# A two-block sequence model in f32 on one core: the attention stage with two heads on row halves, the rotated part on row strips, and score groups set between transposes and value products

## The chip, the cores and the metric

One Trainium2 chip, one of its cores. The metric is the device time of one execution in microseconds (us), the median of several runs. All data are f32. Engines: PE (TensorE: matmuls and transposes; PEld is its weight load), DVE (VectorE), ACT (ScalarE), POOL (GpSimd), SP (the queue that issues most DMAs). Every f32 matmul stands in the trace as two records of PE (two passes over the same columns) and two of PEld; a transpose is one record of each.

## The reference, cut to what matters

The program runs two layers one after the other over 2048 tokens of width 1024. The first (two gated linear recurrences, a gated merge) and the second layer's gates, spatial mixing and output product are not touched. The change is in the second layer's causal attention: 8 heads, 64 plain and 32 rotated channels for each query and key (96 in all), 64 channels of value.

```python
q = einsum('bsr,re->bse', rmsnorm(c_q, q_norm_g), w_uq).reshape(b, s, 8, 96)
q_nope, q_rope = q[..., :64], rope(q[..., 64:], positions)
kv = einsum('bsr,re->bse', rmsnorm(c_kv, kv_norm_g), w_ukv).reshape(b, s, 8, 128)
k_nope, val = kv[..., :64], kv[..., 64:]
k_r = broadcast(rope(k_rope, positions), 8 heads)      # one rotated key for all heads
qf, kf = concat([q_nope, q_rope]), concat([k_nope, k_r])
# for each block of queries:
sc = einsum('bqhd,bkhd->bhqk', qf, kf) / sqrt(96)
sc = where(kpos <= qpos, sc, -inf)
p = softmax(sc); o = einsum('bhqk,bkhd->bqhd', p, val)
```

## The kernel before

`build` calls one phase after another; each ends before the next begins. `phase_latents` makes the latent vectors of queries and keys (`cqT`, `ckvT`), the rotated queries (to memory, `queries_rotated`), the rotated key and the values `vall`. `phase_attention` follows, then `phase_output`.

`phase_attention` takes the heads in four pairs `a`. For a pair it projects the 64 plain channels of queries and keys of both heads (L3302, L3306: 4 blocks of 512 tokens) into PSUM banks; ACT copies each head's 64 rows to rows 0 to 63 of `qT` and `kT` (L3379). Rows 64 to 95 hold the rotated part: of `qT` by DMA (L3285), of `kT` written by DVE in `phase_latents` (L3161, twice per block). So one matmul over 96 rows makes one score tile.

A block `p` (0 to 7) of a pair is 256 query rows: two heads `e` by two row tiles `r` of 128, against 2p+1+r chunks of 128 keys. Two pieces of work belong to a block:

- scores, "S": for each of the four tiles (`TILES`), its keys in pieces of up to 512. PE makes a piece in one of three banks (`NS`, L3319); DVE scales it into `sc` and keeps the row maximum (L3439), adds the mask to the last 128 keys (L3444), and forms the maximum (L3448, L3451). ACT then takes the exponential of the whole tile in place, with its row sum (L3388).
- the rest, "R": for each chunk of keys PE transposes the four 128x128 squares into one of three banks (`NTB`, L3334); DVE or ACT copies the bank to `pT` (L3462, L3399); PE multiplies the values by it, one head on output columns 0 to 63 and the other on 64 to 127 (L3347). Transposes go in groups of four chunks (`GROUP`); the value products of a group follow the transposes of the next. At the end PE spreads the reciprocal sums over the columns (L3361), ACT copies them (L3405) and DVE scales the output (L3464).

The order is a list written by hand, the same for all engines: per pair the projections, then S of block 7, R of the previous pair's block 3, S 0, R 7, S 6, R 0, S 1, R 6, S 5, R 1, S 2, R 5, S 4, R 2, S 3, R 4. A large block's S is followed by a small block's S and so on, so that DVE and ACT work on one block while PE works through another. Which engine copies a transposed chunk is set by `by_vector`: DVE for all chunks of blocks 0 to 3 and the odd chunks of 4 to 7, ACT for the even ones.

"Switch" is used below for a point at which PE goes from matmuls on the whole array to matmuls on a part of its rows or columns, or back, or from one such part size to another.

Of the kernel before, what the change touches and what calls it, by code (L numbers as in the profile page):

```python
# [18 lines left out]
P = 128  # L19
BANK = 512  # L20
# [2889 lines left out]
def phase_latents(chip, hT, positions, inv_freq, w_in, w_uq, q_norm_g, kv_norm_g, cqT, ckvT, kT, qr_d, WV, w_ukv, wv_saved, vall,  # L2910
# [9 lines left out]
    with ExitStack() as st:  # L2920
# [24 lines left out]
        D = Stages(sem("dve_stage"), "vq vkv inv q0 q1 kv krc krs kr0 kr1")  # L2945
# [146 lines left out]
        def _(dve):  # L3092
# [43 lines left out]
            for b in range(NB):  # L3136
# [5 lines left out]
                if b:  # L3142
                    dve.wait_ge(D.sem, D.at(b - 1, "kr1"))
# [16 lines left out]
                for e in range(2):  # L3160
                    dve.tensor_tensor(kT[R, e, t], kr[R, 0, :], kr[R, 1, :], ALU.add).then_inc(D(f"kr{e}"), 1)  # L3161
# [3 lines left out]
def phase_attention(chip, cqT, ckvT, kT, w_uq, w_ukv, qr_d, qr_stored, vall, oT, extra, w_out, wo_saved):  # L3165
# [6 lines left out]
    NS, NTB = 3, 3  # L3172
    GROUP = 4
    NPT = 2 * GROUP
    SC0, TB0, OB0 = 0, 3, 6
    BIG, SMALL = QT // 2 - 1, QT // 4 - 1
    with ExitStack() as st:
# [4 lines left out]
        qT = sb("qT", [QK, 2, SEQ])  # L3182
        ahead = sb("ahead", [P, P])
        sc = [sb("sc_big", [P, 2, (4 * BIG + 3) * P]), sb("sc_small", [P, 2, (4 * SMALL + 3) * P])]
# [5 lines left out]

        order = []
        for a in range(PAIRS):
            order += [("P", a, 0), ("S", a, 7)] + ([("R", a - 1, 3)] if a else [])
            order += [(x, a, p) for x, p in (("S", 0), ("R", 7), ("S", 6), ("R", 0), ("S", 1), ("R", 6), ("S", 5), ("R", 1),
                                            ("S", 2), ("R", 5), ("S", 4), ("R", 2), ("S", 3), ("R", 4))]
        order.append(("R", PAIRS - 1, 3))
        TILES = [(e, r) for e in range(2) for r in range(2)]
        slot = lambda p: 0 if p > SMALL else 1
        length = lambda p, r: 2 * p + 1 + r
        pieces = lambda p, r: (length(p, r) + 3) // 4  # L3200
        chunks = lambda p: range(2 * p + 2)

        score_names, turn_names = [], []
        for x, a, p in order:
            if x == "P":
                score_names += [f"{k}{a}_{b}" for b in range(NB) for k in "qk"]
            elif x == "S":
# [38 lines left out]
        def wait_evicted(eng, name):  # L3246
            done = DT if turned_of[name] else AT
            eng.wait_ge(done.sem, done.at(0, name))
# [576 lines left out]
```

## Time and profile before

| what | value |
|---|---|
| median of 3 runs | 3966.22 us (3966.11 to 3969.06) |
| profiled execution: span from first to last instruction (no other time of it is given) | 3966.9 us |
| PE busy over the span | 3738.9 us, 94% |
| attention stage, first projection to last output scaling | 3142.95 to 3748.7 us |
| DVE, ACT busy in 3146 to 3752 | 366.5 us, 267.8 us of 606 |
| one pair of heads in the middle of the stage | 149.7 us |

The page gives the busy time of each engine and the groups of instructions; a busy PE record holds the time through the array as well, so records overlap and their starts tell more than their lengths. A row of the timeline merges records of one line; its start is that of the first. The granted clock of TensorE (PEclk, 1.00 is 2.4 GHz, 0.50 is 1.2 GHz) stands in the rows by stretch.

### The profile page before, as it was taken

What the parts mean: (1) busy time and instruction counts of PE and PEld (TensorE: products, weight loads), DVE (VectorE), ACT (ScalarE), POOL (GpSimd) and SP (SyncE); (2) the same over time, 40 slices, a digit from 0 to 9 for tenths busy, and PEclk for the clock granted to TensorE, in tenths of its full rate; (3) what the DMA queues carried; (4) which work ended last, traced back from release to release, by engine and by line L of the source; (5) the groups of instructions that cost most, each with busy time, mean ns of one, the idle gap of its engine ahead of it and who ended that gap; (6) DMA issues with size and microseconds to landing.
All of it is one profiled execution on the core that took longest, in us unless ns stands there. A gap on an engine that the chain in (4) does not pass through costs nothing. (4 is left out here: it accounts for less than half of the span.)

```text
span 3966.9 us, 48763 instructions
## 1 busy us (share of the span) xinstructions
PE 3738.9 (94%) x18907; PEld 1965.7 (50%) x18907; DVE 2256.9 (57%) x3731; ACT 1188.3 (30%) x2336; POOL 791.0 (20%) x714
## 2 busy tenths in 40 slices
PE   6999899999899999999999989899999999999898
PEld 3444454444577774444444434344554365565543
DVE  6688426644466666533227767523555465665578
ACT  3333133455355544511110001111231344444300
POOL 0000000000566655311214332223110000000032
PEclk8999999999999999999999999999999999999999
DMA  5122664476655545411325624321111100000133
GB/s 192 48 48 52 114 132 118 110 132 118 161 183 172 169 138 175 162 34 64 117 85 180 212 101 138 106 85 64 48 38 35 33 1 8 8 1 6 69 117 111
DMA packets 590681, 385.27 MB, mean 97 GB/s; under 512 B 414084, under 2 KB 526824, under 8 KB 587508
## 3 DMA queue, kind: packets, MB, share of 16 engines
q1 hardware_dynamic: 573587, 314.52, 28.8%
q0 software_dynamic: 10336, 42.47, 2.9%
q10 hardware_dynamic: 6528, 25.17, 1.6%
q8 instruction: 151, 2.47, 0.3%
q14 instruction: 79, 0.64, 0.1%
HBM read 251.28 MB, written 130.55 MB: 96 GB/s over the span
## 5 line engine op out<-in xcount | busy, mean ns | idle before, releaser
L667 PE MATMUL bank<-uT,front_W 128*128 128x512 f32 (+1 forms) x1216 | 489.6, 564 | 4.6 <-ACT front_b_ L874 4.6
L599 PE MATMUL bank<-uT,front_W 128*128 128x512 f32 (+1 forms) x896 | 363.6, 564 | 0.0
L667 PEld LDWEIGHTS bank<-uT,front_W 128*128 128x128 f32 x1216 | 232.7, 192 | 253.0 <-issue 246.4
L599 PEld LDWEIGHTS bank<-uT,front_W 128*128 128x128 f32 x896 | 170.0, 191 | 183.2 <-issue 179.9
L3319 PE MATMUL bank<-kT,attn_qT 96*128 96x512 f32 (+3 forms) x640 | 248.4, 540 | 7.4 <-ACT kT L3379 6.8
L1357 POOL TENSOR_TENSOR scan_U<-scan_U,gla_w 128x512 f32<-128x512 f32 x144 | 146.7, 1039 | 168.4 <-DVE scan_U L1545 168.4
L3319 PEld LDWEIGHTS bank<-kT,attn_qT 96*128 96x128 f32 x640 | 114.1, 190 | 130.8 <-issue 74.3
L1768 PE MATMUL bank<-gates_T,gates_S 128*128 128x512 f32 x384 | 172.7, 592 | 0.6 <-POOL uT L1730 0.6
L3439 DVE TENSOR_SCALAR_CACHE_REDUCE attn_sc_big<-bank 128x512 f32<-128x512 f32 (+1 forms) x208 | 125.9, 627 | 73.3 <-PE bank L3319 71.4
L3462 DVE COPY attn_pT<-bank 128x512 f32<-128x512 f32 (+1 forms) x184 | 110.3, 635 | 70.8 <-PE bank L3334 70.8
L1347 POOL TENSOR_TENSOR front_work<-front_work,eGl 128x512 f32<-128x512 f32 x144 | 146.6, 1039 | 10.1 <-DVE front_work L1564 3.6
L3553 POOL TENSOR_TENSOR out_S<-uT,out_b 128x512 f32<-128x512 f32 x8 | 13.1, 1638 | 670.1 <-DVE uT L3633 670.1
L3388 ACT ACTIVATE attn_sc_big<-attn_sc_big,attn_top 128x1920 f32<-128x1920 f32 (+3 forms) x64 | 104.3, 1629 | 111.2 <-DVE attn_top L3451 111.2
L1044 DVE RECIPROCAL front_q<-front_q 128x2048 f32<-128x2048 f32 (+1 forms) x8 | 110.0, 13752 | 47.5 <-ACT front_q L821 47.5
L3347 PE MATMUL bank<-attn_pT,uT 128*64 128x256 f32 (+1 forms) x1152 | 129.9, 372 | 5.2 <-DVE attn_pT L3462 5.2
L1768 PE MATMUL bank<-uT 128*128 128x512 f32 x288 | 130.1, 601 | 4.4 <-PEq L1218 4.4
L514 POOL TENSOR_TENSOR front_work<-front_neg_beta,ctri 128x256 f32<-128x256 f32 x18 | 13.1, 751 | 593.9 <-DVE front_neg_beta L1100 510.4
L1834 ACT ACTIVATE gates_r<-gates_r 128x1024 f32<-128x1024 f32 x48 | 50.5, 1053 | 270.1 <-DVE gates_r L1919 267.6
L1564 DVE TENSOR_TENSOR front_work<-front_work,bank 128x512 f32<-128x512 f32 x144 | 92.6, 685 | 63.4 <-PE bank L1439 63.4
L1768 PE MATMUL bank<-uT,WM 128*128 128x512 f32 x288 | 128.0, 592 | 0.0
L1036 DVE SCALAR_TENSOR_TENSOR front_work<-front_work,front_taps 128x2308 f32<-128x2308 f32 (+1 forms) x48 | 121.6, 2533 | 1.7
L3334 PE MATMUL bank<-ident,attn_sc_big 128*128 128x128 f32 x800 | 103.3, 280 | 15.8 <-DVE attn_pT L3462 12.5
(568 smaller groups left out, 7129.1 us busy)
## 6 DMA issues: line engine op xcount, KB each, us to landing
merge_gates<-gates_r ACTq DMA_DIRECT2D x16, 1024.0 KB, 4.1
uT<-merge_gates SPq DMA_DIRECT2D x16, 1024.0 KB, 10.8
gla_asks_keys_values<-front_a SPq DMA_DIRECT2D x14, 1152.0 KB, 10.5
front_W<-in_w_in SPq DMA_DIRECT2D x28, 512.0 KB, 10.6
uT<-in_w_in SPq DMA_DIRECT2D x13, 1024.0 KB, 5.3
scan_dq<-delta_qkv SPq DMA_DIRECT2D x16, 768.0 KB, 5.9
front_work<-gla_asks_keys_values SPq DMA_DIRECT2D x16, 768.0 KB, 7.4
front_work<-delta_qkv SPq DMA_DIRECT2D x16, 768.0 KB, 6.1
```

The costliest lines, as they stand in the source:

```text
L599: m = pe.matmul(bank[:, conv_bank(f, b), 0:n], W[:, f % 2, k, :], uT[:, k, t0:t0 + n], start=(k == 0), stop=(k == KT - 1))
L667: mm = pe.matmul(bank[:, b, 0:n], W[:, s, k, :], uT[:, k, t0:t0 + n], start=(k == 0), stop=(k == KT - 1))
L1036: dve.scalar_tensor_tensor(out=acc[:, lo:WIDE], in0=raw[:, f % 2, lo + t:t + WIDE], scalar=tap[:, t:t + 1], in1=acc[:, lo:WIDE], op0=ALU.m ...
L1044: dve.reciprocal(inv[:, r], inv[:, r]).then_inc(DY("inv"), 1)
L1347: nc.gpsimd.tensor_tensor(SP[d][:], S[d][:], bcast(gl, 2, P), ALU.mult).then_inc(GS(f"SP{d}"), 1)
L1357: nc.gpsimd.tensor_tensor(U[d][:], U[d][:], bcast(w, 2, P), ALU.mult).then_inc(GU(f"U{d}"), 1)
L1768: mm = pe.matmul(bank[:, spot(v, name), :], left[:, k, :], right[:, k, :], start=(k == 0), stop=(k == H - 1))
L3319: pe.matmul(bank[:, SC0 + ring[name] % NS, 0:hi - lo], qT[:, e, i * P:(i + 1) * P], kT[0:QK, e, lo:hi], start=True, stop=True).then_inc(TS ...
L3347: m = pe.matmul(bank[e * DV:(e + 1) * DV, ob, r0:2 * P], vall[:, c, h * DV:(h + 1) * DV], pT[:, n % NPT, e, r0:2 * P], start=(c == 0), sto ...
L3388: act.activation(t, t, ACT.Exp, bias=top[:, slot(p), u], accum_out=total[:, slot(p), u]).then_inc(AE(f"e{a}_{p}_{e}{r}"), 1)
L3439: m = dve.tensor_scalar(t[:, g * BANK:g * BANK + w], bk[:, 0:w], SCALE, None, ALU.mult, ALU.max, accum_out=mx[:, s, u, plain:plain + 1])
L3462: dve.tensor_copy(*turned_spot(a, p, c)).then_inc(DT(name), 1)
```

## The change

The stage keeps its pairs, blocks, tiles, exponentials, transposes and value products, and computes the same scores in two steps. The plain part lies with head 0 on rows 0 to 63 and head 1 on rows 64 to 127 of `qT` and `kT` (one ACT copy of 128 rows for each projected block). The rotated part lies in `qR` and `kR` on four strips of 32 rows, one for each tile (head, row tile); DVE writes the rotated key four times in `phase_latents`, and four DMAs bring the rotated queries of a pair. A group of four scores (two heads, two row tiles, the same 512 keys) takes four matmuls over 64 rows and then four over 32 rows that add to the same four banks (`SC0` 0 to 3). Transposes have two banks (`NTB`), which the projections share; `pT` has seven slots.

The blocks go 7, 6, ..., 0 in each pair, and the rest of the block before stands between the score groups of a block: a group of scores, two chunks transposed, two chunks of values, two transposed, two of values, the next group. Projections are spread: the key blocks ahead of block 7's groups, the query blocks ahead of blocks 7, 5, 3 and 1. ACT makes all four exponentials of a block after that block's last group ("E"), and copies most transposed chunks; DVE copies the second half of a rest's last group and whole groups that find no score group beside them.

```diff
-        NS, NTB = 3, 3
+        NTB = 2
...
-    NPT = 2 * GROUP
-    SC0, TB0, OB0 = 0, 3, 6
+    NPT = 7
+    SC0, TB0, OB0 = 0, 4, 6
...
-        qT = sb("qT", [QK, 2, SEQ])
+        qT, kT = sb("qT", [P, SEQ]), sb("kT", [P, SEQ])
+        qR = sb("qR", [P, HALF, P])
...
+        def rest_items(b, k, by_vector):
+
+            a, p = b
+            now, before = groups(p)[k], groups(p)[k - 1] if k else []
+            for h in range(0, max(len(now), len(before)), 2):
+                for c in now[h:h + 2]:
+                    order.append(("T", a, p, c, by_vector or (h > 0 and k == len(groups(p)) - 1)))
+                for c in before[h:h + 2]:
+                    order.append(("V", a, p, c))
+
+        def rest_end(b):
+
+            order.extend(("V", *b, c) for c in groups(b[1])[-1])
+            order.append(("H", *b))
+        for i, (a, p) in enumerate(blocks):
+            prev = blocks[i - 1] if i else None
+            of_rest = len(groups(prev[1])) if prev else 0
+            for k in range(max(pieces(p), of_rest)):
+                if k < pieces(p):
+                    order += [("P", a, *x) for x in ahead_of.get((p, k), [])]
+                    order.append(("S", a, p, k))
+                if k == 0 and i > 1:
+                    order.append(("O", *blocks[i - 2]))
+                if k < of_rest:
+                    rest_items(prev, k, k >= pieces(p))
+                if k == pieces(p) - 1:
+                    order.append(("E", a, p))
+            if prev:
+                rest_end(prev)
...
+            def score(a, p, g):
+                n = score_at[a, p, g]
+                if g == 0:
+                    wait_evicted(pe, f"q{a}_{p // 2}")
+                if p == TOP:
+                    wait_evicted(pe, f"k{a}_{g}")
+                    if g == 0:
+                        pe.wait_ge(r_loaded, 64 * (a + 1))
+                keys = lambda r: slice(g * BANK, min((g + 1) * BANK, length(p, r) * P))
+                spot = lambda e, r: bank[:, SC0 + 2 * r + e, 0:keys(r).stop - keys(r).start]
                 for e, r in TILES:
+                    if n:
+                        b, q, f = scores[n - 1]
+                        pe.wait_ge(DM.sem, DM.at(0, f"s{b}_{q}_{f}_{e}{r}"))
+                    i, rows = 2 * p + r, slice(e * NOPE, (e + 1) * NOPE)
+                    pe.matmul(spot(e, r), qT[rows, i * P:(i + 1) * P], kT[rows, keys(r)], start=True, stop=False)
+                for e, r in TILES:
+                    rows = slice((2 * e + r) * ROPE, (2 * e + r + 1) * ROPE)
+                    pe.matmul(spot(e, r), qR[rows, p, :], kR[rows, keys(r)], start=False, stop=True,
+                              tile_position=((2 * e + r) * ROPE, 0)).then_inc(TS(f"s{a}_{p}_{g}_{e}{r}"), 1)
...
-                for e in range(2):
-                    dve.tensor_tensor(kT[R, e, t], kr[R, 0, :], kr[R, 1, :], ALU.add).then_inc(D(f"kr{e}"), 1)
+                for n in range(P // ROPE):
+                    dve.tensor_tensor(kR[n * ROPE:(n + 1) * ROPE, t], kr[R, 0, :], kr[R, 1, :], ALU.add).then_inc(D(f"kr{n}"), 1)
```

PE in the kernel before, from the rest of block 7 to the first scores of block 5 (L3334 transposes, L3347 value products, L3361 shares, L3319 scores; a piece of up to 512 keys per score):

```order
L3334 MATMUL bank<-ident,attn_sc_big 128x128 x32
L3347 MATMUL bank<-attn_pT,uT 64x256 x8
L3334 MATMUL bank<-ident,attn_sc_big 128x128 x16
L3347 MATMUL bank<-attn_pT,uT 64x256 x8
L3334 MATMUL bank<-ident,attn_sc_big 128x128 x14
L3347 MATMUL bank<-attn_pT,uT 64x256 x14
L3347 MATMUL bank<-attn_pT,uT 64x128 x2
L3361 MATMUL bank<-ident,attn_share 64x128 x4
L3319 MATMUL bank<-kT,attn_qT 128x512 x3
L3319 MATMUL bank<-kT,attn_qT 128x128
```

PE in the changed kernel, in block 6 with the rest of block 7 (L3349 plain part on row halves, L3352 rotated part on strips, L3362 transposes, L3374 value products):

```order
L3349 MATMUL bank<-attn_kT,attn_qT 128x512 x4
L3352 MATMUL bank<-kR,attn_qR 128x512 x4
L3362 MATMUL bank<-ident,attn_sc_odd 128x128 x8
L3374 MATMUL bank<-attn_pT,uT 64x256 x4
L3362 MATMUL bank<-ident,attn_sc_odd 128x128 x8
L3374 MATMUL bank<-attn_pT,uT 64x256 x4
L3349 MATMUL bank<-attn_kT,attn_qT 128x512 x4
L3352 MATMUL bank<-kR,attn_qR 128x512 x4
L3362 MATMUL bank<-ident,attn_sc_odd 128x128 x8
L3374 MATMUL bank<-attn_pT,uT 64x256 x4
```

Scores, which stood in one run ahead of or behind a rest, now stand in groups of four between half groups of transposes and value products; the number of switches in the stage, counted over this order, goes from 111 to 388 (80 of them into row halves, 80 into strips).

ACT in the kernel before, around the exponentials of block 6 (L3399 copies of transposed chunks, L3388 exponentials, L3405 spread shares):

```order
L3399 ACTIVATE attn_pT<-bank 128x512 x4
L3405 ACTIVATE attn_spread<-bank 128x256
L3388 ACTIVATE attn_sc_big,attn_total<-attn_sc_big,attn_top 128x1664
L3388 ACTIVATE attn_sc_big,attn_total<-attn_sc_big,attn_top 128x1792
L3388 ACTIVATE attn_sc_big,attn_total<-attn_sc_big,attn_top 128x1664
L3388 ACTIVATE attn_sc_big,attn_total<-attn_sc_big,attn_top 128x1792
L3405 ACTIVATE attn_spread<-bank 128x256
```

ACT in the changed kernel at the same place (L3418 copies, L3411 exponentials, L3424 spread shares, L3404 copies of a projection):

```order
L3418 ACTIVATE attn_pT<-bank 128x512 x14
L3411 ACTIVATE attn_sc_even,attn_total<-attn_sc_even,attn_top 128x1664 x2
L3411 ACTIVATE attn_sc_even,attn_total<-attn_sc_even,attn_top 128x1792 x2
L3424 ACTIVATE attn_spread<-bank 128x256
L3404 ACTIVATE attn_qT<-bank 128x512
L3418 ACTIVATE attn_pT<-bank 128x512 x12
```

The query projection of block 5, which PE needs for its next scores, stands on ACT behind the exponentials of block 6 and the spread shares.

## Rows read from the trace of the kernel before

**Rows 1.** Stretches: the attention stage and one middle pair (busy us by engine, records).

```profile
core 0: us, PE busy (x) PEld busy (x) DVE busy (x) ACT busy (x) POOL busy (x), PEclk, DMA share, GB/s
3146.00:3752.00 606.00, 565.66 (x3229) 343.24 (x3228) 366.50 (x1208) 267.79 (x457) 0.00 (x0) 0.99 0.03 7
3467.91:3617.63 149.72, 140.62 (x808) 85.42 (x809) 91.57 (x303) 66.58 (x115) 0.00 (x0) 1.00 0.02 4
```

**Rows 2.** PE's transposes by shape, 3146 to 3752: busy, mean ns, idle before.

```profile
L3334 PE MATMUL bank<-ident,attn_sc_big 128*128 128x128 f32 x800 | 103.3, 280 | 15.8 <-DVE attn_pT L3462 12.5 <-ACT attn_pT L3399 1.7 <-ACT attn_sc_big L3388 1.2
```

**Rows 3.** Waits summed over 3140 to 3760: who waited, for whom, us, times, longest.

```profile
ACT attn_sc_big L3388 <- DVE attn_top L3451: 111.2, 64, 6.5
PEld bank L3334 <- DVE attn_pT L3462: 31.0, 51, 1.5
PEld bank L3319 <- DVE attn_sc_big L3439: 23.2, 79, 0.5
```

**Rows 4.** Timeline of a pair's first scores: PE's weight loads, DVE's first piece.

```profile
start us, us, engine line op out<-in xcount [idle before <-releaser]
...
3158.35 0.19 PEld L3319 LDWEIGHTS bank<-kT,attn_qT 96*128 96x128 f32 x1 [0.24 <-issue]
3158.78 0.19 PEld L3319 LDWEIGHTS bank<-kT,attn_qT 96*128 96x128 f32 x1 [0.24 <-issue]
...
3159.09 0.69 DVE L3439 TENSOR_SCALAR_CACHE_REDUCE attn_sc_big<-bank 128x512 f32<-128x512 f32 x1 [21.49 <-PE bank L3319]
```

**Rows 5.** Timeline of PE in a rest: value products on column halves.

```profile
3248.83 1.95 PE L3347 MATMUL bank<-attn_pT,uT 128*64 128x256 f32 x16
3250.71 1.78 PE L3334 MATMUL bank<-ident,attn_sc_big 128*128 128x128 f32 x14
3252.42 3.46 PE L3347 MATMUL bank<-attn_pT,uT 128*64 128x256 f32 x32
3255.71 0.61 PE L3361 MATMUL bank<-ident,attn_share 128*64 128x128 f32 x8
```

**Rows 6.** Timeline of PE in the scans of the first layer: strips of 32 rows.

```profile
1202.05 0.73 PE L1470 MATMUL bank<-scan_gv,scan_kmt 32*128 32x128 f32 x16
1202.71 0.30 PE L1413 MATMUL bank<-front_work 128*32 128x128 f32 x2
...
1204.29 0.27 PE L1377 MATMUL bank<-ident,scan_gq 128*128 128x128 f32 x1
1204.40 0.27 PE L1378 MATMUL bank<-ident,scan_gq 128*128 128x128 f32 x1
```

**Rows 7.** Timeline of DVE: a tile's last piece, then the next tile.

```profile
3161.34 0.42 DVE L3439 TENSOR_SCALAR_CACHE_REDUCE attn_sc_big<-bank 128x256 f32<-128x256 f32 x1
...
3162.41 0.68 DVE L3439 TENSOR_SCALAR_CACHE_REDUCE attn_sc_big<-bank 128x512 f32<-128x512 f32 x1
3163.06 0.69 DVE L3439 TENSOR_SCALAR_CACHE_REDUCE attn_sc_big<-bank 128x512 f32<-128x512 f32 x1
```

**Rows 8.** ACT's groups by shape, 3146 to 3752.

```profile
L3399 ACT ACTIVATE attn_pT<-bank 128x512 f32<-128x512 f32 x104 | 61.8, 595 | 119.5 <-PE bank L3334 119.4
L3388 ACT ACTIVATE attn_sc_big<-attn_sc_big,attn_top 128x2048 f32<-128x2048 f32 x8 | 16.0, 2002 | 12.6 <-DVE attn_top L3451 12.6
L3388 ACT ACTIVATE attn_sc_big<-attn_sc_big,attn_top 128x1920 f32<-128x1920 f32 x8 | 15.2, 1896 | 23.5 <-DVE attn_top L3451 23.5
L3388 ACT ACTIVATE attn_sc_big<-attn_sc_big,attn_top 128x1792 f32<-128x1792 f32 x8 | 14.3, 1789 | 9.9 <-DVE attn_top L3451 9.9
L3388 ACT ACTIVATE attn_sc_big<-attn_sc_big,attn_top 128x1664 f32<-128x1664 f32 x8 | 13.5, 1683 | 19.0 <-DVE attn_top L3451 19.0
```

**Rows 9.** Stretches around the second pair's first scores; PEclk is the granted clock.

```profile
3299.00:3301.90 2.90, 1.21 (x4) 0.55 (x4) 0.00 (x0) 1.77 (x3) 0.00 (x0) 1.00 0.33 68
3301.90:3305.30 3.40, 3.40 (x6) 1.34 (x5) 1.40 (x4) 0.00 (x0) 0.00 (x0) 0.50 0.00 0
```

**Rows 10.** The line that writes the rotated key in the phase before.

```profile
L3161 DVE TENSOR_TENSOR kT<-latents_work x8: 676/680/683, 3031.4 to 3129.4; 32x512 f32<-32x512 f32 x8
```

More of the change, by code:

```diff
@@ L3197, in phase_attention @@
[L3197 to L3207, printed above, removed]
-                score_names += [f"s{a}_{p}_{e}{r}_{g}" for e, r in TILES for g in range(pieces(p, r))]
-            else:
-                turn_names += [f"t{a}_{p}_{c}" for c in chunks(p)]
@@ L3211, in phase_attention @@
[L3211 removed]
+        TILES = [(e, r) for r in range(2) for e in range(2)]
+        slot = lambda p: p % 2
+        length = lambda p, r: 2 * p + 1 + r
+        pieces = lambda p: (p + 2) // 2
+        groups = lambda p: [list(range(2 * p + 2))[c:c + GROUP] for c in range(0, 2 * p + 2, GROUP)]
+        blocks = [(a, p) for a in range(PAIRS) for p in range(TOP, -1, -1)]
+        ahead_of = {(TOP, 0): [("q", 3), ("k", 0)], (TOP, 1): [("k", 1)], (TOP, 2): [("k", 2)], (TOP, 3): [("k", 3)],
+                    (5, 0): [("q", 2)], (3, 0): [("q", 1)], (1, 0): [("q", 0)]}
@@ new lines, in phase_attention @@
+        for k in range(len(groups(0))):
+            order.append(("O", *blocks[-2]))
+            rest_items(blocks[-1], k, False)
+        rest_end(blocks[-1])
+        order.append(("O", *blocks[-1]))
+        scores = [it[1:] for it in order if it[0] == "S"]
+        score_names = [f"s{a}_{p}_{g}_{e}{r}" for a, p, g in scores for e, r in TILES]
+        score_at = {x: n for n, x in enumerate(scores)}
+        ring_names = [f"t{it[1]}_{it[2]}_{it[3]}" if it[0] == "T" else f"{it[2]}{it[1]}_{it[3]}" for it in order if it[0] in "TP"]
@@ new lines, in valued @@
+            def valued(a, p, c):
+                name = f"t{a}_{p}_{c}"
+                wait_evicted(pe, name)
+                if c == 0 and rests.index((a, p)) >= 2:
+                    pe.wait_ge(DO.sem, DO.at(0, "o%d_%d" % rests[rests.index((a, p)) - 2]))
+                r0 = 0 if c < length(p, 0) else P
+                for e in range(2):
+                    h = 2 * a + e
+                    m = pe.matmul(bank[e * DV:(e + 1) * DV, out_bank(a, p), r0:2 * P], vall[:, c, h * DV:(h + 1) * DV],
+                                  pT[:, turn[name] % NPT, e, r0:2 * P], start=(c == 0), stop=(c == 2 * p + 1))
+                m.then_inc(TO(name.replace("t", "o")), 1)
@@ L3421, in _, with score @@
             dve.wait_ge(mask_ready, 2)
-            def scores(a, p):
+            def score(a, p, g):
                 s = slot(p)
-                old = [ap for x, *ap in order[:order.index(("S", a, p))] if x == "R" and slot(ap[1]) == s]
-                if old:
-                    b, q = old[-1]
+                i = blocks.index((a, p))
+                if g == 0 and i >= 2:
+                    b, q = blocks[i - 2]
                     dve.wait_ge(TT.sem, TT.at(0, f"t{b}_{q}_{2 * q + 1}"))
```

286 lines of the change are left out of this document (122 added, 164 removed).

## The prediction

> **What bounds the kernel now.** I read the stretches first [rows 1]. In the attention stage PE is busy 565.7 of 606 us, DVE 366.5, ACT 267.8; a middle pair of heads takes 149.7 us with PE busy 140.6 of it, at full clock. So PE's stream sets the pace, and a change counts by PE's own work and by what PE waits for. The groups and the summed waits come second: PE's transposes stood idle 15.8 us in the whole stage [rows 2], its score weights waited 23.2 us for DVE in 79 pieces of at most 0.5 us [rows 3]. ACT's 111.2 us of waiting for row maxima [rows 3] cost nothing by themselves, as ACT has room. Third come the timelines, where starts (not the overlapping lengths) tell what PE needs for a piece of work.
>
> **PE's prices.** One record of 512 columns follows the next after 0.43 us [rows 4], so 384 take 0.32, 256 take 0.216 and 128 take 0.11 (two transposes lie 0.11 apart [rows 6]). Work on two column halves runs side by side: 16 records of 256 columns take 1.88 us to the next line [rows 5], which is 8 x 0.216 and 0.15 left over. The 32 records behind them (four of only 128 columns, in matmuls of the second row tile) take 3.29 = 14 x 0.216 + 2 x 0.11 + 0.05, and there the next line stays on column halves. So a switch costs about 0.15, as 14 transposes say too (1.71 = 14 x 0.11 + 0.17). Four strips of 32 rows run side by side: 16 records of 128 columns take 0.66 us = 4 x 0.11 + 0.22 [rows 6], so I give a switch around strips 0.2. No row shows halves of 64 rows or a switch from halves to strips. The bounds: row halves pair up as column halves do, or don't at all; the switch costs 0, or 0.2. I take pairing and 0.2, the values of the nearest rows.
>
> **Scores on PE.** A pair of heads has 20 groups of four scores: 12 of four full pieces, 4 of two times 384 and two times 512 columns, 4 of two times 128 and two times 256. Before, one group took 8 records in a row: 8 x 0.43 = 3.43, then 3.0 and 1.30; a pair 12 x 3.43 + 4 x 3.0 + 4 x 1.30 = 58.4. After, the plain part takes 4 x 0.43 = 1.71 (1.50, 0.65), the rotated part 2 x 0.43 = 0.86 (0.86, 0.43), and two switches 0.4: 2.97, 2.76, 1.48; a pair 52.6. That is 5.8 us less: packing alone would save 13.8 us, and 40 switches take 8 of them back.
>
> **Other switches.** Transposes use the whole array and value products its column halves. Before, a pair changes between them or to scores some 28 times (111 in the stage), after it does 57 times beside those into halves and strips. 29 x 0.15 = 4.4 us more. The rest stays as it is: 272 transposes of 0.11 (29.9 us), value products of 256 records of 256 and 32 of 128 columns, two side by side (128 x 0.216 + 16 x 0.11 = 29.4), 24 projection records of 0.43 (10.3), 64 records of the spread sums, side by side (3.5). PE's own time in a pair: 135.7 before, 134.2 after.
>
> **Waits.** Before, a pair holds 149.7 - 135.7 = 14.0 us in which PE stands. Those of after must be built up. Five places come out:
>
> (a) Block 7 has almost no rest beside it (the two chunks of the former pair's block 0), so its groups 1 to 3 stand behind one another with one key projection between. All four scores end together behind the strips. DVE then starts after 0.31 [rows 4] and takes one piece each 0.65 [rows 7]: the fourth bank is free after 0.31 + 4 x 0.65 + 0.06 = 2.97; the fourth plain score (0.96 with its switch) and the strips (1.06) follow: 5.0 a group where PE's own work is 2.97 + 0.86 + 0.15 = 3.98. Three times 1.02 is 3.1. The first group waits for ACT's copy of its keys (0.595 [rows 8] + 0.31: 0.9), and the second key projection for one of two transpose banks (1.1, an estimate from two copies of 0.595). Sum 5.1.
>
> (b) The first transposes of block 7 need all four exponentials, which ACT now makes only behind the last group: the first maximum comes 0.31 + 1.07 after it (from a tile's last piece to the next tile [rows 7]), then 2 x 1.90 + 2 x 2.00 [rows 8]: 9.2. PE reaches them after block 6's first group, which itself is held by DVE's four last pieces (0.31 + 3 x 1.07 + 0.9, and 2.0 of its own): 6.4. Wait 2.8. Before, the small blocks' work lay there. In the later blocks the rest of two blocks earlier covers it (four halves of a group, over 7 us).
>
> (c) With two transpose banks instead of three, the third of the first four chunks of each rest, which have no value products between, waits for the copy of the first: 0.44 + 0.31 + 0.595 + 0.06 = 1.4 against 1.0 when PE gets there. Seven blocks x 0.4 = 2.8.
>
> (d) The query projections ahead of blocks 5, 3 and 1 stand on ACT behind exponentials and spread shares (the order of ACT above). Block 5: 1.38 + 2 x 1.68 + 2 x 1.79 [rows 8] + spread 0.4 + copy 0.6 + hand-over 0.3 = 9.6, while PE has the half group of transposes, the last value products, the sums and the projection: 7.5. Wait 2.1. In blocks 3 and 1 exponentials are done, and the latency of the copy remains, 0.9 each. Sum 3.9.
>
> (e) DVE copies the last two chunks of a rest; in blocks 2 and 0 and at a pair's start these copies queue behind four tiles' last pieces (4 x 1.07). An estimate of 1.3 at two places: 2.6.
>
> Sum 17.2: a pair takes 134.2 + 17.2 = 151.4, 1.7 more than before, four pairs 7 us.
>
> **What costs nothing.** One copy of 128 rows in place of two of 64 saves ACT time that it has. Four DMAs in place of two stand on SP's queue ahead of the next pair's weights; in the stage the DMA engines are 3% busy [rows 1], and the wait for them stands once a pair, a whole pair after issue; without that cover a pair's start would wait some microseconds. DVE takes the same score pieces as before and is busy 366.5 of 606 us [rows 1], so its total doesn't set the end; where its order matters stands under (a) and (e). **What costs little.** The rotated key is written four times, not twice: 8 more of 0.68 us [rows 10]. Three blocks lie under PE's work, the last lies near the end of the phase: 0.7 us or nothing. **Clock.** The second pair's start shows the granted clock at 0.50 for 3.40 us behind a stretch in which PE was busy 1.21 of 2.90 [rows 9]; such a stretch costs half, 1.7. The waits in (b) are of that length in four places; I add two such stretches, 3.4 us (from 0 to 6.8).
>
> **Sum.** 7 + 0.7 + 3.4 = 11 over the profiled span of 3966.9, which lies 0.7 above the median of the runs, so 3977 to 3978. I take 3978.
>
> **The rivals.** *The switch from halves to strips is free.* Both stay on rows, and the 80 switches of 0.2 fall off: 16 us less, 3962, no change to be told. For it: no row shows that switch. Against it: each change of part in rows 5 and 6 cost something. The Trainium skill (TensorEngine Tiling (Array Packing), Key Properties) says that a change of tiling mode drains the engine while one of the tile alone does not; by that the switch is paid in full and the forecast stands, and rows 5 agree for column halves (0.15 with, 0.05 without).
>
> *The new order hides waits (faster).* My waits were added one by one, as though PE came to each with nothing gained from the last. If (b), (d) and (e) vanish because PE arrives late, with score groups between half rests giving ACT and DVE time everywhere, 9.3 us a pair go, up to 37 in all, and the two slow stretches: 3938 with all, 3955 with half. The mechanism decides from PE's arrival 2 to 3 us later than I counted. For it: before, transposes and scores waited in 130 pieces of 0.4 us on average [rows 3], which wider spacing should remove.
>
> *Full packing.* If plain and rotated part cost a half and a quarter of 58.4 and no switch costs anything, a pair's scores take 43.8 and PE's own time is 135.7 - 14.6 = 121.1; with 17.2 of waits 138.3, 11.4 less than now, four times 46: 3925. Rows 5 and 6 speak against it, since switches show there. The Trainium skill gives that factor (the same page, Theoretical Speedup: up to 2x for 64, up to 4x for 32); side by side the rows agree, the switches are what it leaves out.
>
> *The clock falls at every wait of 2 us or more.* Two a pair, (b) and (d), eight of them at 1.7 to 3.4 us in place of my 3.4: 3988 to 4002. Rows 9 show it once.
>
> *Row halves don't pair.* The change then doesn't do what it says: the plain part takes 12 x 3.43 + 4 x 3.0 + 4 x 1.30 instead of half of it, 29.2 us a pair more, 4095.
>
> **How the numbers follow.** A measurement of this kernel can tell about 0.2%, 8 us. The forecast, 3970 to 3990 by itself, has 0.47; the free switch 0.22; hidden waits 0.20; full packing 0.03; the clock 0.06; no pairing 0.02. Faster: 0.20 + 0.03 = 0.23. Same: 0.22 and 0.05 of the forecast's lower end, 0.27. Slower: 0.42 + 0.06 + 0.02 = 0.50. The range leaves out full packing, no pairing, half of the hidden waits and a little of the clock: 3945 to 4000.
>
> **What would show it.** In the profile after, the timeline of a full group in the middle of a rest: eight records of the plain part in 1.7 us, then 0.2, then 0.86 for the strips; a shorter step between them is the first rival. The groups of the plain part: 3.4 us a group means no pairing. The idle time ahead of block 7's groups, of its first transposes and of the scores of block 5: 1, 2.8 and 2.1 us; if they are far smaller, the second rival holds, and a pair takes 140 to 146 us instead of 151. PE's share of busy time should fall. Half-clock stretches: five, not ten. The forecast is wrong if a wait that I haven't listed comes in each block: 1 us in each of 8 blocks and four pairs would be 32 us.

## The result and the profile after

The changed kernel takes 3983.68 us (median of 4 runs, 3979.25 to 3986.64) and the kernel before 3967.64 us beside it: a ratio of 1.0040, 95% interval 1.0026 to 1.0054. The change makes the kernel 16 us slower. The profiled execution, the shortest of the four, spans 3977.5 us.

The stage first. These are stretches of the changed kernel (us; busy us and records of PE, PEld, DVE, ACT, POOL; granted clock; DMA): the whole stage, two middle pairs of heads, and the turn from one pair to the next.

```profile
3139.20:3759.50 620.30, 566.54 (x3872) 303.81 (x3872) 280.28 (x1080) 307.59 (x553) 0.00 (x0) 0.98 0.03 7
3321.39:3475.91 154.52, 141.06 (x968) 75.69 (x969) 70.01 (x270) 76.49 (x139) 0.00 (x0) 0.98 0.02 6
3475.91:3629.51 153.60, 140.14 (x968) 75.20 (x969) 70.09 (x270) 76.49 (x139) 0.00 (x0) 0.99 0.02 6
...
3317.50:3320.00 2.50, 0.16 (x4) 0.00 (x0) 2.33 (x13) 2.15 (x3) 0.00 (x0) 1.00 0.00 0
3320.00:3326.80 6.80, 5.41 (x20) 2.41 (x24) 1.27 (x7) 5.95 (x7) 0.00 (x0) 0.50 0.00 0
3477.00:3480.40 3.40, 3.40 (x12) 1.21 (x12) 0.00 (x0) 3.40 (x5) 0.00 (x0) 0.50 0.00 0
```

The stage took 605.8 us before (3142.95 to 3748.73) and takes 620.3 now, 14.5 more; a pair takes 153.6 or 154.5 where [rows 1] had 149.7. Behind PE's wait at a pair's start the clock is granted at 0.50 for 3.4 or 6.8 us. Such stretches lie at the start of the stage and of each pair, five in all, and take 23.8 us of the stage; before there were three, with 12.2 us of it. The clock's share is at most half of the difference, 5.8 us (less where PE would have waited at full clock too). The rest is 8.7 us, or 2.2 us a pair. The parts of the program ahead of the stage, of which the change touches only the writes of the rotated key, ran 3.8 us shorter in this execution, so the spans differ by less than the medians.

PE's waits in one pair (who waited, for whom: us, times, longest):

```profile
PE bank L3381 <- DVE attn_share L3479: 3.7, 1, 3.7
PE bank L3349 <- ACT attn_qT L3404: 3.2, 3, 1.7
PE bank L3349 <- ACT attn_kT L3404: 3.0, 4, 0.8
PE bank L3362 <- ACT attn_pT L3418: 2.0, 8, 0.3
PE bank L3374 <- DVE attn_pT L3475: 1.0, 1, 1.0
PE bank L3328 <- ACT attn_pT L3418: 0.6, 1, 0.6
```

L3381 spreads the row sums, L3349 makes the plain scores, L3362 the transposes, L3374 the value products, L3328 the keys. These were PE's largest waits inside the stage of the kernel before (four pairs):

```profile
PE bank L3334 <- DVE attn_pT L3462: 20.2, 26, 1.3
PE bank L3319 <- ACT kT L3379: 6.8, 4, 1.7
PE bank L3347 <- DVE attn_pT L3462: 5.2, 4, 1.3
```

PE waited for DVE's copies of transposed chunks and, once a pair, for ACT's copy of the keys. New are the waits for the reciprocal, for ACT's copies of the queries, and for keys three more times a pair; the waits for banks of transposes now come from ACT. A wait counted here ends where the weight load starts; from the last column of the work before it is some 0.1 to 0.2 us longer, and those gaps are used below.

The timeline of PE in the middle of a rest shows PE's prices:

```profile
3337.00 1.99 PE L3349 MATMUL bank<-attn_kT,attn_qT 64*128 64x512 f32 x8
3338.92 1.14 PE L3352 MATMUL bank<-kR,attn_qR 32*128 32x512 f32 x8
3339.99 1.09 PE L3362 MATMUL bank<-ident,attn_sc_odd 128*128 128x128 f32 x8
3341.01 1.08 PE L3374 MATMUL bank<-attn_pT,uT 128*64 128x256 f32 x8
3342.03 1.09 PE L3362 MATMUL bank<-ident,attn_sc_odd 128*128 128x128 f32 x8
```

The eight plain records take 1.92 us, which is 1.71 and a switch of 0.21; the strips take 1.07 us, which is 0.86 and 0.21. Two chunks transposed take 1.02 (0.88 and 0.14), two chunks of values 1.02 (0.86 and 0.16). So a group takes 2.99 us; row halves pair, and the switch from halves to strips is paid.

The turn of a pair, PE, DVE and ACT, from the last strips of block 7 on:

```profile
3315.72 1.14 PE L3352 MATMUL bank<-kR,attn_qR 32*128 32x384 f32 x8
3316.67 0.42 DVE L3454 TENSOR_SCALAR_CACHE_REDUCE attn_sc_odd<-bank 128x256 f32<-128x256 f32 x1 [2.05 <-PE bank L3352]
3316.79 0.87 PE L3374 MATMUL bank<-attn_pT,uT 128*64 128x256 f32 x8
...
3317.85 1.90 ACT L3411 ACTIVATE attn_sc_odd<-attn_sc_odd,attn_top 128x1920 f32<-128x1920 f32 x1 [4.03 <-DVE attn_top L3468]
...
3321.17 0.17 DVE L3479 RECIPROCAL attn_share<-attn_total 128x4 f32<-128x4 f32 x1
3321.39 1.12 PE L3381 MATMUL bank<-ident,attn_share 128*64 128x128 f32 x8 [3.73 <-DVE attn_share L3479]
...
3323.61 1.99 ACT L3411 ACTIVATE attn_sc_odd<-attn_sc_odd,attn_top 128x2048 f32<-128x2048 f32 x1
...
3327.52 1.09 PE L3362 MATMUL bank<-ident,attn_sc_odd 128*128 128x128 f32 x8
```

The sums of the former pair's block 0 need a reciprocal of 0.17 us (L3479), which stands on DVE behind the four last pieces of block 7. PE stands from 3317.50 to 3321.39 for it, 3.89 us. The exponentials end at 3325.6; the transposes that need them come at 3327.5, since the scores between them ran at half clock.

### The profile page after: what moved, and what is told of

It is laid out like the page before. It is cut to its first block and busy times, and to the rows that moved or that the text cites. A ratio compares the mean times of both kernels' runs of the same rounds, so it can differ in the third digit from the quotient of the medians.

```text
span 3977.5 us, 50060 instructions
## 1 busy us (share of the span) xinstructions
PE 3731.5 (94%) x19547; PEld 1922.9 (48%) x19547; DVE 2177.1 (55%) x3611; ACT 1228.8 (31%) x2432; POOL 791.4 (20%) x714
## 3 DMA queue, kind: packets, MB, share of 16 engines
q1 hardware_dynamic: 577555, 314.52, 28.6%
## 5 line engine op out<-in xcount | busy, mean ns | idle before, releaser
L3454 DVE TENSOR_SCALAR_CACHE_REDUCE attn_sc_odd<-bank 128x512 f32<-128x512 f32 (+2 forms) x160 | 91.5, 606 | 191.6 <-PE bank L3352 191.6
L3418 ACT ACTIVATE attn_pT<-bank 128x512 f32<-128x512 f32 x232 | 125.3, 591 | 220.9 <-PE bank L3362 220.9
L3349 PE MATMUL bank<-attn_kT,attn_qT 64*128 64x512 f32 (+3 forms) x640 | 147.7, 572 | 25.1 <-ACT attn_qT L3404 12.5
L3374 PE MATMUL bank<-attn_pT,uT 128*64 128x256 f32 (+1 forms) x1152 | 139.6, 376 | 4.6 <-DVE attn_pT L3475 4.0
L3454 DVE TENSOR_SCALAR_CACHE_REDUCE attn_sc_even<-bank 128x512 f32<-128x512 f32 (+1 forms) x128 | 69.6, 586 | 103.3 <-PE bank L3352 103.3
L1768 PEld LDWEIGHTS bank<-gates_T,gates_S 128*128 128x128 f32 x384 | 72.3, 190 | 89.3 <-issue 87.3
L781 ACT ACTIVATE front_work<-bank 128x512 f32<-128x512 f32 (+1 forms) x56 | 31.7, 566 | 226.5 <-PE bank L599 226.5
```

What stands on the lines that cost most here:

```text
L1768: mm = pe.matmul(bank[:, spot(v, name), :], left[:, k, :], right[:, k, :], start=(k == 0), stop=(k == H - 1))
L3349: pe.matmul(spot(e, r), qT[rows, i * P:(i + 1) * P], kT[rows, keys(r)], start=True, stop=False)
L3374: m = pe.matmul(bank[e * DV:(e + 1) * DV, out_bank(a, p), r0:2 * P], vall[:, c, h * DV:(h + 1) * DV], pT[:, turn[name] % NPT, e, r0:2 * P] ...
L3418: act.activation(*turned_spot(a, p, c), ACT.Copy).then_inc(AT(name), 1)
L3454: m = dve.tensor_scalar(t[:, g * BANK:g * BANK + w], bk[:, 0:w], SCALE, None, ALU.mult, ALU.max, accum_out=mx[:, s, u, g:g + 1])
```

## The experiments

Line numbers shift by up to five between the kernels; names of tiles tell what a row is.

**The 3.9 us at a pair's start.** Is it a wait of its own, or does the next one stand behind it? Only the place of the reciprocal on DVE is changed:

```diff
                     order.append(("S", a, p, k))
+                if p == TOP and k == 1 and i:
+                    order.append(("F", *prev))
...
-                elif x == "H":
+                elif x == "F" or x == "H" and (at[1] or at[0] == PAIRS - 1):
                     shares(*at)
```

> The changed kernel with one edit: at the start of pairs 2 to 4, DVE makes the reciprocal shares of the former pair's block 0 after block 7's second score group, not behind the four last pieces of block 7. Theory (the place is a chain, not one wait): the 3.9 us that PE stands at L3381 go, but PE then stands 2.5 to 3.5 us ahead of block 7's first transposes, because ACT's exponentials end 9.2 us after the last score group whatever DVE does; time within 4 us of the changed kernel (3980 to 3988 beside 3984). Rival (the 3.9 us are a wait of its own): three times 3.9 us and three half-clock stretches fall off, 3964 to 3970.

Measured: 3983.26 us (ratio 1.0039, 1.0025 to 1.0052), the same as the changed kernel. The wait moved as the theory said. PE's timeline at the same place:

```profile
3322.29 0.61 PE L3383 MATMUL bank<-ident,attn_share 128*64 128x128 f32 x8
3322.82 3.88 PE L3351 MATMUL bank<-attn_kT,attn_qT 64*128 64x512 f32 x8
3326.64 1.14 PE L3354 MATMUL bank<-kR,attn_qR 32*128 32x512 f32 x8
3330.53 1.09 PE L3364 MATMUL bank<-ident,attn_sc_odd 128*128 128x128 f32 x8 [2.76 <-ACT attn_sc_odd L3413]
```

The sums come at once, the next scores wait for their banks (3.82 us for a plain part that takes 1.92), and the transposes stand 2.92 us for the exponentials. What sets the time there is the chain from the last score group over DVE's first maximum and ACT's 7.7 us of exponentials (3317.85 to 3325.59 in the changed kernel).

**The waits for projections.** The query projections of blocks 5, 3 and 1 go into block 7, where PE waits anyway:

```diff
-        ahead_of = {(TOP, 0): [("q", 3), ("k", 0)], (TOP, 1): [("k", 1)], (TOP, 2): [("k", 2)], (TOP, 3): [("k", 3)],
-                    (5, 0): [("q", 2)], (3, 0): [("q", 1)], (1, 0): [("q", 0)]}
+        ahead_of = {(TOP, 0): [("q", 3), ("k", 0)], (TOP, 1): [("k", 1), ("q", 2)], (TOP, 2): [("k", 2), ("q", 1)],
+                    (TOP, 3): [("k", 3), ("q", 0)]}
```

> The changed kernel with one edit: the query projections of blocks 5, 3 and 1 stand behind the key projections ahead of block 7's groups 1 to 3. Theory (term d of the prediction is a wait for ACT's copies, and block 7's groups wait for DVE anyway): per pair the waits of 1.8 + 0.9 + 0.9 us at the first scores of blocks 5, 3, 1 go, the three of 0.9 us in block 7 go as well (the query projection of 1.7 us covers the copy of the keys), 6.3 us a pair, 25 us in all: 3955 to 3964. Rival (the waits move on, since DVE or ACT is late there anyway): less than 8 us, 3976 to 3986.

Measured: 3955.07 us (0.9968, 0.9956 to 0.9981), 28.6 less than the changed kernel and 12 less than the kernel before. Of PE's waits over the stage the largest that are left, but for one of 4.1 us for weights at the stage's start, are these:

```profile
PE bank L3381 <- DVE attn_share L3479: 11.2, 3, 3.7
PE bank L3362 <- ACT attn_pT L3418: 7.6, 31, 0.3
PE bank L3374 <- DVE attn_pT L3475: 4.0, 4, 1.0
PE bank L3349 <- ACT attn_kT L3404: 3.1, 4, 0.8
```

The waits for queries are gone, and of those for keys four remain (the first group of each pair). PE's gaps in a pair fall from 16.4 us to 10.0, as the theory had it. The rest of the 28.6 is about what the clock gives back, half of the difference between 23.8 us of the stage at half clock and 17.1. So one table of places, the copies' latency behind projections made just in time, is worth more than the whole loss of the change.

**The third transpose bank.** One bank for outputs instead of two frees a third for transposes:

```diff
-    NTB = 2
+    NTB = 3
...
-    SC0, TB0, OB0 = 0, 4, 6
+    SC0, TB0, OB0 = 0, 4, 7
...
-        out_bank = lambda a, p: OB0 + rests.index((a, p)) % 2
+        out_bank = lambda a, p: OB0
...
-                if c == 0 and rests.index((a, p)) >= 2:
-                    pe.wait_ge(DO.sem, DO.at(0, "o%d_%d" % rests[rests.index((a, p)) - 2]))
+                if c == 0 and rests.index((a, p)) >= 1:
+                    pe.wait_ge(DO.sem, DO.at(0, "o%d_%d" % rests[rests.index((a, p)) - 1]))
```

> The changed kernel with three banks for transposes and projections and one bank, not two, for the outputs of the rests. Theory (term c: the third transposed chunk of a rest waits 0.41 us for a bank): seven waits of 0.41 us a pair go, 11.6 us in all: 3969 to 3975. Rival (the single output bank makes PE's first value product wait for DVE's output scaling, which stands behind score pieces): a new wait of over 1 us at each rest, 3985 to 4010.

> The three edits of share_early, q_in_gaps and three_banks together. If the waits add up, as PE's stream sets the pace: 25 + 12 and 0 to 12 from the early shares, 3935 to 3948, which is under the kernel before. If they overlap (what one edit frees, the next wait takes): 3955 to 3970.

Measured: three_banks 3989.78 us (1.0055, 1.0042 to 1.0067), all_three 3955.00 (0.9968, 0.9955 to 0.9980). The theory fell for the first and the rival held: every wait for a transpose bank is gone, and the first of these stands in their place over the stage of three_banks (the other two are those of the changed kernel):

```profile
PE bank L3374 <- DVE uT L3483: 17.0, 8, 2.3
PE bank L3349 <- ACT attn_qT L3404: 12.5, 12, 1.7
PE bank L3349 <- ACT attn_kT L3404: 11.9, 16, 0.8
```

DVE's output scaling (uT, L3483) stands behind the score pieces of blocks 1 and 0, and the value products now wait for it, eight times. Six of these eight waits are followed by a half-clock stretch of 3.4 us, and the stage has 37.5 us at half clock where the changed kernel has 23.8. In all_three the sum over the edits failed at this term (2.43 and 2.16 us a pair) and at the early shares (2.91 us a pair for the exponentials).

So the scaling goes ahead of those score pieces, beside the edits of q_in_gaps and three_banks:

```diff
+                if k == 0 and i > 1 and p <= 1:
+                    order.append(("O", *blocks[i - 2]))
                 if k < pieces(p):
...
-                if k == 0 and i > 1:
+                if k == 0 and i > 1 and p > 1:
                     order.append(("O", *blocks[i - 2]))
```

> The edits of q_in_gaps and three_banks together, and DVE's output scaling set ahead of the score pieces of blocks 1 and 0, where three_banks showed PE waiting 2.4 and 2.2 us a pair for it. Theory (the third bank is worth the seven waits of 0.41 us a pair as soon as the output bank comes free in time): 11.6 us less than q_in_gaps and the 1.2 us at the value products of block 2 as well, 3955 - 12 to 16: 3939 to 3944. Rival (the output wait only moves, since the scaling then waits for ACT behind the exponentials and holds up the score pieces): 3950 to 3960.

Measured: 3945.72 us (0.9942, 0.9928 to 0.9955), 9.4 less than q_in_gaps, a little short of the 12 to 16 expected: the last copies by DVE still hold value products eight times. The third bank is worth about what term (c) of the prediction gave (2.8 us a pair, 11 in all), once the other bank's work is in time: PE's gaps fall from 10.0 to 6.9 us a pair.

**Order or packing?** The same order with whole-array scores; these kernels sum both heads' plain rows and leave the rotated part out, so that a score costs one full pass over its keys, as long as the 96-row matmul:

```diff
-                    i, rows = 2 * p + r, slice(e * NOPE, (e + 1) * NOPE)
-                    pe.matmul(spot(e, r), qT[rows, i * P:(i + 1) * P], kT[rows, keys(r)], start=True, stop=False)
-                for e, r in TILES:
-                    rows = slice((2 * e + r) * ROPE, (2 * e + r + 1) * ROPE)
-                    pe.matmul(spot(e, r), qR[rows, p, :], kR[rows, keys(r)], start=False, stop=True,
-                              tile_position=((2 * e + r) * ROPE, 0)).then_inc(TS(f"s{a}_{p}_{g}_{e}{r}"), 1)
+                    i = 2 * p + r
+                    pe.matmul(spot(e, r), qT[:, i * P:(i + 1) * P], kT[:, keys(r)], start=True, stop=True
+                              ).then_inc(TS(f"s{a}_{p}_{g}_{e}{r}"), 1)
```

> The changed kernel's order with the packing taken away: each score is one matmul over all 128 rows of qT and kT (both heads' plain rows summed, the rotated part left out), as long on PE as the 96-row matmul of the kernel before; no strips. PE's own time alone says 5.8 us a pair more than the changed kernel, 4007. Theory (the packed form ends its four scores together and so makes DVE late; whole matmuls end one by one, and waits of 2 to 4 us a pair at the pair's start fall off): 3988 to 4002. Rival (packing brings nothing, its switches eat it): 3984 or less.

> three_banks_early with the packing taken away as in whole_array (one matmul of 128 rows a score, both heads' plain rows summed, the rotated part left out). PE's own time says 5.8 us a pair, 23 us more than three_banks_early: 3969. Theory (the packed form's late, common end of four scores costs waits only at a pair's start, 2.1 us and a half-clock stretch, and 2 us at the small blocks): packing is worth 6 to 14 us here, 3952 to 3960. Rival (it is worth no more than the 3 us of whole_array): 3944 to 3950.

Measured: whole_array 3986.96 us (1.0047, 1.0034 to 1.0060), whole_array_in_best 3941.46 us (0.9938, 0.9925 to 0.9950). So the changed kernel's order alone, with scores as long on PE as before, costs some 20 us. Packing takes 3 us off in that order; in that of three_banks_early the whole array is 4 us ahead. In both cases the intervals of packed and whole overlap, so neither difference is shown. whole_array lies just below the theory's range, whole_array_in_best 10 us below it and under the rival's too. First a full group, then a pair, of whole_array_in_best; below them a pair of three_banks_early:

```profile
3329.32 3.70 PE L3351 MATMUL bank<-attn_kT,attn_qT 128*128 128x512 f32 x8
3332.85 1.04 PE L3361 MATMUL bank<-ident,attn_sc_odd 128*128 128x128 f32 x8
```

```profile
3315.67:3458.94 143.27, 140.08 (x808) 84.32 (x809) 73.58 (x270) 75.83 (x139) 0.00 (x0) 1.00 0.02 6
```

```profile
3317.76:3461.44 143.68, 137.42 (x969) 76.18 (x969) 70.21 (x270) 75.99 (x139) 0.00 (x0) 0.99 0.02 6
3317.40:3320.90 3.50, 3.15 (x14) 1.79 (x16) 0.27 (x3) 3.50 (x5) 0.00 (x0) 0.51 0.00 0
```

A whole group takes 3.53 us, the packed one 2.99: PE does save. But this pair takes the same, and the next one 145.2 us packed, with 6.8 us at half clock, and 143.3 whole. In the packed pair PE's gaps of over 0.3 us come to 3.89 at the pair's start, 0.74 and 1.33 at the small blocks and 0.96 at the first keys, 6.9; in the other to 1.76, 0.89, 0.96, 3.6. That is 3.3 us, and the half-clock stretch, which only the packed pair has, costs some 1.6 more; together they give back the some 4.6 us that PE saves. The pair's start shows how the packing does it. These are the last group of block 7 and DVE's first piece of it, whole and then packed:

```profile
3310.10 3.17 PE L3351 MATMUL bank<-attn_kT,attn_qT 128*128 128x384 f32 x8
...
3310.95 0.42 DVE L3453 TENSOR_SCALAR_CACHE_REDUCE attn_sc_odd<-bank 128x256 f32<-128x256 f32 x1 [2.52 <-PE bank L3351]
```

```profile
3310.39 1.77 PE L3351 MATMUL bank<-attn_kT,attn_qT 64*128 64x384 f32 x8
...
3313.03 0.42 DVE L3456 TENSOR_SCALAR_CACHE_REDUCE attn_sc_odd<-bank 128x256 f32<-128x256 f32 x1 [2.80 <-PE bank L3354]
```

The four packed scores end together behind the strips, so DVE starts 2.64 us after the group's first record and then has four pieces at once. Whole matmuls end one by one, DVE starts after 0.85 us and works beside them. The reciprocal that PE waits for stands behind these pieces in both kernels. No run made packed scores end one by one, so it isn't shown that this is the whole cause. Nor was a kernel run that makes the model's own scores on the whole array in this order; like the kernel before it would need two ACT copies of 64 rows for a projected block.

**Does the order of the halves matter?** `sorted(TILES)` in the loop of the plain part sets both scores of head 0 ahead of those of head 1:

```diff
-                for e, r in TILES:
+                for e, r in sorted(TILES):
                     if n:
```

> The changed kernel with the four plain scores of a group in another order: both of head 0 (rows 0 to 63), then both of head 1 (rows 64 to 127). Theory (PE takes its queue in order, so halves run side by side only where neighbours lie on different halves): the plain part of a full group takes 3.0 to 3.4 us and not 1.9, 18 to 25 us a pair, 4055 to 4085. Rival (PE's queue looks ahead over four matmuls): 3984.

Measured: 3985.94 us (1.0043, 1.0029 to 1.0057), the same. The theory fell. The eight records still lie side by side (PE's timeline):

```profile
3343.74 1.99 PE L3349 MATMUL bank<-attn_kT,attn_qT 64*128 64x512 f32 x8
3345.67 1.14 PE L3352 MATMUL bank<-kR,attn_qR 32*128 32x512 f32 x8
```

1.93 us as in the changed kernel (1.92), where eight records one after another would take 3.43: PE paired the halves although four records of one stood ahead of the first of the other.

**What does setting groups between the rest bring?** q_in_gaps with a block's groups in one run, then the rest, then the exponentials (the edit also moves 24 of DVE's 56 copies of transposed chunks to ACT):

```diff
-                if k < of_rest:
-                    rest_items(prev, k, k >= pieces(p))
-                if k == pieces(p) - 1:
-                    order.append(("E", a, p))
+            for k in range(of_rest):
+                rest_items(prev, k, False)
+            order.append(("E", a, p))
```

> q_in_gaps with each block's score groups in one run, the former block's rest behind them, and the exponentials behind that rest's copies. Theory (a group alone stands 4.87 us, as block 7 shows, since DVE frees the four banks late; PE's own part of it is 3.0): nine groups a pair are 1.9 us longer, 17 us a pair, 60 to 68 us in all, less 2.5 for 17 fewer switches: 4005 to 4025. Rival (setting groups between the rest brings nothing): 3950 to 3960.

Measured: 4047.39 us (1.0200, 1.0186 to 1.0214), 92 more than q_in_gaps where 50 to 70 were expected. PE and DVE in two groups, and the stretch behind them:

```profile
3343.53 2.96 PE L3348 MATMUL bank<-attn_kT,attn_qT 64*128 64x512 f32 x8 [0.86 <-DVE attn_sc_even L3453]
...
3346.42 1.14 PE L3351 MATMUL bank<-kR,attn_qR 32*128 32x512 f32 x8
3347.58 0.69 DVE L3453 TENSOR_SCALAR_CACHE_REDUCE attn_sc_even<-bank 128x512 f32<-128x512 f32 x1 [1.93 <-PE bank L3351]
...
3348.33 2.96 PE L3348 MATMUL bank<-attn_kT,attn_qT 64*128 64x512 f32 x8 [0.77 <-DVE attn_sc_even L3453]
```

```profile
3354.80:3361.70 6.90, 6.90 (x32) 4.73 (x30) 3.19 (x18) 2.39 (x4) 0.00 (x0) 0.51 0.00 0
```

A group in a run takes 4.80 us, as the theory had it. The stage has 68 us at half clock, where q_in_gaps has 17: up to 26 of the 92 us, and the theory had no term for that. The remaining 66 lie in its 60 to 68.

**Switches.** three_banks_early with four chunks transposed, then four of values:

```diff
-            for h in range(0, max(len(now), len(before)), 2):
-                for c in now[h:h + 2]:
+            for h in range(0, max(len(now), len(before)), 4):
+                for c in now[h:h + 4]:
-                    order.append(("T", a, p, c, by_vector or (h > 0 and k == len(groups(p)) - 1)))
-                for c in before[h:h + 2]:
+                    order.append(("T", a, p, c, by_vector or (c % 4 > 1 and k == len(groups(p)) - 1)))
+                for c in before[h:h + 4]:
```

> three_banks_early with four chunks transposed, then four of values, in place of two and two: 72 switches fewer in the stage (304 for 376). Theory (a switch costs 0.15 us, and with three banks the transposes don't wait for their copies): 10.8 us less, 3933 to 3938. Rival one (a switch costs next to nothing): 3944 to 3947. Rival two (the seven pT slots make the copy of the fourth chunk wait for a value product): 3948 to 3960.

Measured: 3936.33 us (0.9924, 0.9911 to 0.9936), 9.4 less for 72 switches: 0.13 us each, beside the 0.15 of the prediction. PE's gaps of over 0.3 us are the same as in three_banks_early, 6.9 us a pair.

**Work in the wait.** Two query projections fill the place where PE stands for the exponentials of block 7. The run starts from three_banks_early and has the edit of share_early too:

```diff
-        ahead_of = {(TOP, 0): [("q", 3), ("k", 0)], (TOP, 1): [("k", 1), ("q", 2)], (TOP, 2): [("k", 2), ("q", 1)],
-                    (TOP, 3): [("k", 3), ("q", 0)]}
+        ahead_of = {(TOP, 0): [("q", 3), ("k", 0)], (TOP, 1): [("k", 1), ("q", 2)], (TOP, 2): [("k", 2)], (TOP, 3): [("k", 3)]}
...
                     order.append(("S", a, p, k))
+                    if (p, k) == (TOP - 1, 0):
+                        order += [("P", a, "q", 1), ("P", a, "q", 0)]
```

> three_banks_early with the early shares of share_early, and the query projections of blocks 3 and 1 set between block 6's first score group and block 7's first transposes, where PE stands 2.9 us for the exponentials. Theory (work put into that wait is free, 3.7 us of projections fill it; block 7's groups 2 and 3 fall back from 5.7 to 4.9 us): 1 us a pair and three half-clock stretches of 1.7 us less, 3936 to 3942. Rival (ACT copies the projections behind the exponentials, and the transposes' banks wait for that): 3945 to 3952.

> queries_in_the_hole and rest_in_fours together. The one takes a wait and half-clock stretches at a pair's start, the other switches in the middle of a pair, so both should add: 3945.7 - 10.6 - 9.4 = 3925.7, between 3923 and 3929. Rival (the fewer switches only lead PE to a wait at the small blocks or at the pair's start): 3933 to 3937.

Measured: queries_in_the_hole 3935.14 us (0.9921, 0.9908 to 0.9935), with rest_in_fours 3928.89 us (0.9901, 0.9884 to 0.9917). The first gained 10.6, a little more than expected. In PE's timeline of queries_in_the_hole transposes follow projections without a wait, and the stretch that holds this pair's start is at full clock:

```profile
3314.73 3.70 PE L3336 MATMUL bank<-cqT,attn_WQ 128*128 128x512 f32 x8
3318.27 2.06 PE L3367 MATMUL bank<-ident,attn_sc_odd 128*128 128x128 f32 x16
```

```profile
3300.00:3440.00 140.00, 135.84 (x960) 75.50 (x960) 69.33 (x268) 75.76 (x138) 0.00 (x0) 1.00 0.02 6
```

Most of the gain is the clock's: the stage is 9.0 us shorter than in three_banks_early (572.9 for 581.9), and it has 3.4 us at half clock where that has 20.5, worth up to 8.5 us. The wait itself mostly moved: PE's gaps of over 0.3 us fall by 2.1 us a pair, but shorter stalls inside the groups grow by as much (block 6's first plain part takes 2.90 us, not 1.92). The early shares and the new places of the projections were not tried one without the other in this order.

The two edits add up but for 3 us. Within a pair nothing is lost (142.1 us, and 139.9 with rest_in_fours); where the 3 us go isn't settled. The last kernel keeps the change's packed scores and is 1.0% faster than the kernel before, 1.4% faster than the changed one.

## Why the prediction was right

The forecast was 3978 us, 12 above the median of before; 16 were measured, within the 3970 to 3990 that it gave the forecast by itself, and slower as it said.

- **PE's prices** held to 0.02 us: group 2.99 (predicted 2.97), halves in pairs, a switch 0.14 to 0.21. The switch from halves to strips, which no row of before showed, is paid at 0.21; the first rival falls. PE's own time in a pair (without its gaps of over 0.3 us and half of its half-clock time) was put at 134.2 us and measured at 134.7 and 135.5 in the two middle pairs. By the same count the whole scores take 140.8 in this order, so packing saves 5.3 to 6.1 us on PE where 5.8 were predicted; in the order of three_banks_early it is 139.7 and 135.1, 4.6. Small groups gain nothing (1.50 us packed, 1.41 whole).
- **The waits** of a pair sum to 16.4 us, predicted 17.2. (a) was 4.4 for 5.1, but by another releaser: I had three groups wait for DVE's banks, and the trace has three waits of 0.91 us for ACT's copy of the keys just projected. (c) 2.9 for 2.8, seven of 0.42 as worked out; (d) 1.82 + 0.91 + 0.91 = 3.6 for 3.9; (e) 1.5 for 2.6, of which 1.16 stand for DVE's copy and the rest for one of ACT's. (b) was 3.9 for 2.8 and had another face: I had the transposes wait for ACT, but PE stood one step earlier, for a reciprocal behind DVE's last pieces. The share_early run shows both as links of one chain, and the predicted 2.8 us as 2.92 when the first link is taken out. In the first pair, which has no former rest, the transposes waited 2.92 us in the changed kernel too.
- **The clock**: five stretches as forecast, but two of them 6.8 us long; up to 5.8 us for 3.4. The rival with ten stretches falls: (d) stayed under its 2 us, and in three_banks two of the eight waits of 2.2 to 2.4 us were followed by none. **The rotated key** cost nothing to be seen: the stage begins 13.3 us after the start of its last write, before 13.5.
- **Hidden waits** (the second rival): not in the changed kernel, whose gaps sum to nearly what was counted. Its support, 130 waits of 0.4 us, was read off weight loads; PE's own waits before were 26 for DVE's copies and next to none for score banks (0.4 us). But q_in_gaps took 28.6 us out with one table, so the price of that rival, 37 at most, was about the size that a better order can bring.
- **Full packing** falls by the group of 2.99 us; **no pairing** by the halves' 1.92.

Some of the nearness is luck. PE's own time was put 0.5 to 1.3 us a pair too low and the waits 0.8 too high, which cancels, and (a) and (b) came near their sizes partly by waits other than those named.

What I had wrong in reasoning: I set the loss against packing's gain as if they were two things. Against whole_array the packed scores cost 2.8 us a pair more in gaps (16.4 for 13.6) and have 3.4 to 6.8 us at half clock in each middle pair (worth up to 1.7 to 3.4), where whole_array has none; that is most of the 5.3 to 6.1 that packing saves on PE. (a) and (b) did count on four scores ending together, but as a cost of the new order and not of the packing.

What stays open: whether the kernel before would gain from packing in its own order, with three banks for scores and a matmul a tile, and whether packed scores that end one by one would keep PE's gain; neither was tried. Why the clock fell for 3.4 us at one pair's start and 6.8 at another's isn't settled.

## What to carry to other kernels

When you pack several short contractions into the array, ask whether the engine that empties the banks can still start as early as before: here results that end together made the reader 1.8 us late at a pair's start, and the waits and half-clock time that only the packed form had took back about what PE gained. A projection made just ahead of its use costs the latency of its copy each time (0.9 us, 1.8 behind exponentials); set it where PE waits anyway. When a wait is found, take it out alone once: here taking out the first link (3.9 us) brought nothing, and filling the wait with work brought 10.6 us, most of it because the half-clock stretches behind it went.

## What was not expected of the hardware

PE set matmuls on the two row halves side by side although four records on one half stood ahead of the first on the other: 1.93 us for eight records, as with halves alternating. And in runs_of_groups, where PE stood for 0.77 and 0.86 us between groups, the stage had 68 us at half clock for 17 in q_in_gaps, up to 26 of the 92 us that it lost: a wait can cost more than its length.
